# Modulation vectors of the later layers: from TensorE tiles to row sums on VectorE

## The reference, cut to what matters

```
mod_l = silu(c) @ w_mod[l] + b_mod[l]          # l = 0, 1; 1024 x 6144; the context uses c_ctx
sh1, sc1, g1, sh2, sc2, g2 = split(mod_l, 6)   # 1024 values each
h = rmsnorm(x) * (1 + sc1) + sh1
x = x + g1 * rmsnorm(mixer(h))
f = rmsnorm(x) * (1 + sc2) + sh2
x = x + g2 * rmsnorm((silu(f @ w_gate) * (f @ w_up)) @ w_down)
# the second pair of layers: the same with c_2, w_ada_2[0], w_ada_2[1] (1024 x 6144)
# and w_kv_ada_2 (1024 x 2048)
```

## Time and profile before

| | |
|---|---|
| Time, median of 3 runs | 2813.16 us (2807.47 to 2814.35) |
| Profiled execution, first to last instruction | 2812.3 us |
| PE busy | 2681.0 us (95%) |
| DVE busy | 2006.6 us (71%) |
| ACT busy | 1485.3 us (53%) |
| HBM traffic | 239 GB/s over the span |

### The profile page before, as it was taken

The page is one execution under the profiler, slowest core; times in us unless marked ns, Lnnn a source line. Parts: engine busy times, 40 slices in busy tenths (PEclk is TensorE's granted clock), DMA queues, the critical chain, the costliest instruction groups (busy, mean ns, idle before and its releaser), DMA issues.

```text
span 2812.3 us, 33306 instructions
## 1 busy us (share of the span) xinstructions
PE 2681.0 (95%) x13626; PEld 2140.2 (76%) x13626; DVE 2006.6 (71%) x2297; ACT 1485.3 (53%) x1663; POOL 121.7 (4%) x172
## 2 busy tenths in 40 slices
PE   7989999999999889999999999999999999999997
PEld 4767677777776667777777777888888888888886
DVE  4556565456457556558754667799999999999998
ACT  4322465245344244344643445677676677767775
POOL 3023100000000310000000000000000000000000
PEclk9989999999999899999899999999999999999999
DMA  7543556666545365652466433299999999999995
GB/s 272 181 154 120 195 195 213 215 229 215 195 168 192 135 222 197 239 187 72 150 210 235 162 105 116 98 364 368 353 369 365 356 358 366 359 358 361 369 365 206
DMA packets 283021, 674.26 MB, mean 240 GB/s; under 512 B 16774, under 2 KB 113158, under 8 KB 256752
## 3 DMA queue, kind: packets, MB, share of 16 engines
q1 hardware_dynamic: 277088, 664.34, 65.5%
q0 software_dynamic: 4912, 6.67, 0.9%
q10 hardware_dynamic: 864, 1.06, 0.1%
HBM read 670.93 MB, written 1.10 MB: 239 GB/s over the span
## 4 chain that ended last, share of the span: by engine, by line
PE 80%; DVE 10%; ACT 7%; DMA 2%; issue 1%; SPq 0%; POOL 0%; ACTq 0%; DVEq 0%; POOLq 0%
PE psum L560 22%; PE psum L562 21%; PE psum L561 21%; PE psum L76 8%; PE psum L394 3%; DVE wslot_r L570 2%; PE psum L1477 1%; DVE cacc L76 1%; PE psum L3009 1%; DMA first<-in_w_mod 1%; PE psum L1616 1%; PE psum L2041 1%; ACT whi_r L76 1%; DVE x L76 1%; DVE dslot_r L570 1%
## 5 line engine op out<-in xcount | busy, mean ns | idle before, releaser
L560 PE MATMUL psum<-whi_r,xhi_r 128*128 128x512 f32 (+1 forms) x752 | 295.2, 393 | 5.2 <-DVE dslot_r L570 2.1
L570 DVE TENSOR_TENSOR wslot_r<-wslot,whi_r 128x2048 fp32r<-128x2048 f32 (+1 forms) x114 | 255.6, 2252 | 50.1 <-ACT whi_r L76 48.9
L562 PE MATMUL psum<-whi_r,xlo_r 128*128 128x512 f32 (+1 forms) x752 | 288.8, 384 | 0.0
L561 PE MATMUL psum<-wslot_r,xhi_r 128*128 128x512 f32 (+1 forms) x736 | 282.4, 384 | 0.0
L570 DVE TENSOR_TENSOR dslot_r<-dslot,ld_hi_r 128x2048 fp32r<-128x2048 f32 x44 | 100.6, 2292 | 183.3 <-ACT ld_hi_r L76 183.3
L76 ACT ACTIVATE whi_r<-wslot 128x2048 fp32r<-128x2048 f32 (+1 forms) x114 | 212.2, 1874 | 23.5 <-DVE wslot L76 6.2
L570 DVE TENSOR_TENSOR ring_r<-ring,wide_r 128x2048 fp32r<-128x2048 f32 x84 | 192.0, 2288 | 18.1 <-ACT wide_r L2968 17.2
L570 DVE TENSOR_TENSOR wslot_r<-wslot,arena_r 128x2048 fp32r<-128x2048 f32 x85 | 194.2, 2288 | 14.3 <-ACT arena_r L2968 13.0
L570 DVE TENSOR_TENSOR wslot_r<-wslot,wide_r 128x2048 fp32r<-128x2048 f32 x83 | 189.7, 2288 | 17.0 <-ACT wide_r L2968 16.3
L570 DVE TENSOR_TENSOR ring_r<-ring,arena_r 128x2048 fp32r<-128x2048 f32 x84 | 191.7, 2287 | 12.9 <-ACT arena_r L2968 11.6
L2968 ACT ACTIVATE arena_r<-wslot 128x2048 fp32r<-128x2048 f32 x85 | 163.1, 1919 | 66.9 <-PE psum L562 60.1
(11 more groups left out here) (535 smaller groups left out, 6382.1 us busy)
## 6 DMA issues: line engine op xcount, KB each, us to landing
wslot<-in_moe_w_gate SPq DMA_DIRECT2D x29, 2048.0 KB, 7.9
ring<-in_moe_w_down SPq DMA_DIRECT2D x29, 2048.0 KB, 7.7
wslot<-in_moe_w_up SPq DMA_DIRECT2D x28, 2048.0 KB, 8.0
ring<-in_moe_w_up SPq DMA_DIRECT2D x28, 2048.0 KB, 8.1
ring<-in_moe_w_gate SPq DMA_DIRECT2D x27, 2048.0 KB, 7.9
wslot<-in_moe_w_down SPq DMA_DIRECT2D x27, 2048.0 KB, 7.7
dslot<-in_w_mod SPq DMA_DIRECT2D x35, 1024.0 KB, 4.8
wslot<-in_w_gate SPq DMA_DIRECT2D x66, 512.0 KB, 5.5
```

The costliest lines, as they stand in the source:

```text
L560: t.matmul(out_, hi, w_hi, start=start, stop=False)
L561: t.matmul(out_, hi, w_lo, start=False, stop=False)
L562: return t.matmul(out_, lo, w_hi, start=False, stop=stop)
L570: return v.tensor_tensor(one_pass(lo), src, one_pass(hi), ALU.subtract)
```

## The change

Of the 13 tiles the first five stay on PE: mod0 whole and the first two of mod1. The last third of mod1 (the scale and gate of the second half of layer 1, image tokens only, since the context is not updated there), ada0, kv and ada1 become 16 blocks of 1024 features. Their weights come from the host transposed: `w_dots` holds, for output feature p*8+k of a block, its 1024 weights in one row. On the chip one `tensor_tensor_reduce` on DVE multiplies 128 such rows by the conditioning vector, which stands on all partitions (`cond`, in the memory of stage), and sums along each row: one column of a block, 8 a block, 128 in all, each on 512 KB of weights.

A step of a dense line does two of them ahead of the first `beside` and two after the split of the first half of the tokens. The first line does 64, the second and third 32 each. The conditioning vector is broadcast by a POOL transfer and passed through Silu on ACT, once for c and once for c_2. The bias is added at the end of a block; gates go to DRAM as before. Nothing replaces the calls of `mod_step` in layer 1's projections, mixer and output projection.

```diff
+    def dot(limit):
+        n = dot_next[0]
+        if n not in dot_there or not broad[2]:
+            return
...
+        slot.reader = ve.put(v.tensor_tensor_reduce, slot.ap[:], slot.ap[:], cond, 1.0, 0.0, ALU.mult, ALU.add, column[:, k:k + 1],
+                             after=[dot_there.pop(n), broad[2]])
+        fetch_dot(limit)
+        if k == KD - 1:
...
+            summed = ve.op(v.tensor_tensor, column, column, dot_bias[:, n // KD, :], ALU.add)
...
+        if n == 2 * KD - 1:
+            broadcast_condition(i["c_2"][0])
...
+    def fetch_dot(limit):
+        n = dot_asked[0]
+        if n < limit:
+            dot_asked[0] += 1
+            slot = dot_slots[n % 2]
+            sp.wait(slot.reader)
+            nc.sync.dma_start(slot.ap[:], dot_rows[n // KD, :, n % KD, :]).then_inc(slot.sem, 16)
...
-    mod_tiles = [(job, j) for job in jobs for j in range(job[3])]
+    mod_tiles = [(job, j) for job in jobs[:2] for j in range(job[3])][:5]
...
-            def modulate(n):
+            def condition(n):
                 if n == 0:
-                    own_slot[0], line_slot.reader, allow_ahead[0] = line_slot, self.up_[0, 1], False
-                elif n > 1:
-                    while at_step[0] and mod_step() and at_step[0][0] != "half":
-                        pass
...
+                    for slot in dot_slots:
+                        slot.reader = self.up_[0, 1]
+                        fetch_dot(self.dots)
+                elif n < end - 1:
+                    for _ in range(2):
+                        dot(self.dots)
...
+                if n:
+                    condition(n)
                 beside(n)
-                if n:
-                    modulate(n)
                 self.up(n, 1)
                 self.high_w(n + 1, 1)
+                shape_condition()
                 self.gate(n, 1)
...
                 self.split_h(n, 0)
-                if n == 0:
-                    modulate(0)
+                condition(n)
                 beside(n)
...
         rounded = [high_part(0, half) for half in range(2)]
-        mod_step()
         low_part(0, 0, rounded[0])
-        settle()
+        if l == 0:
+            while mod_step():
+                pass
+            broadcast_condition(i["c"][0])
...
     finish_off(c0)
-    for _ in range(3):
-        mod_step()
     finish_off(c1)
```

More of the change, by code:

```diff
@@ L507, in load_columns @@
         for which, tile, at_ in parts:
-            mod_until(job, tile)
+            while (job, tile) not in known_cols:
+                assert mod_step()
             cols_for[which] = col_of[job][:, at_]
@@ L513, in ask_gates @@
     def ask_gates(job, *uses):
-        mod_until(job, 2 if max(blk for s, blk in uses) == 5 else 1)
+        while (job, 2 if max(blk for s, blk in uses) == 5 else 1) not in stored:
+            assert mod_step()
         grow_of.extend((job, s, blk) for s, blk in uses)
@@ L695, in build @@
     ld_hi = [at(f"ld_hi{u}", 16384 + 2048 * u, 2048) for u in range(2)]
-    line_slot = Slot(nc, "s_mod", at("mod_half", 18432, 2048))
+    dot_slots = [Slot(nc, f"s_dot{u}", at(f"dot{u}", 18432 + 1024 * u, 1024)) for u in range(2)]
+    s_broad, s_dotrow = nc.alloc_semaphore("s_broad"), nc.alloc_semaphore("s_dotrow")
+    cond = stage[:].rearrange("p u n -> p (u n)")
+    dot_gate = sb("dot_gate", [P, 2, 64])[:, :, 0:KD]
+    dot_there, dot_rows_n, gate_out, broad = {}, [0, 0], [None, None], [0, None, None]
@@ new lines, in build, with broadcast_condition, shape_condition @@
+    dot_next, dot_asked = [0], [0]
+    def broadcast_condition(src):
+        po.wait(*turned_out, (s_kept[0], kept_n[0]), (s_kept[1], kept_n[1]), ve.now())
+        nc.gpsimd.dma_start(cond, src.partition_broadcast(P)).then_inc(s_broad, 16)
+        broad[0] += 16
+        broad[1], broad[2] = (s_broad, broad[0]), None
+    def shape_condition():
+        if broad[1]:
+            broad[2] = ac.put(a.activation, cond, cond, ACT.Silu, after=[broad[1]])
+            broad[1] = None
+    def fetch_dot(limit):
[5 more added lines that the diff above has]
+            nc.sync.dma_start(slot.ap[:], dot_rows[n // KD, :, n % KD, :]).then_inc(slot.sem, 16)
+            slot.n += 16
+            dot_there[n] = (slot.sem, slot.n)
@@ L2627, in build @@
     cat4, keep, fetched = joint_mix(0)
-    line = Line(i["w_gate"][0], i["w_up"][0], i["w_down"][0], 2, whi, [keep, fetched[0]])
+    line = Line(i["w_gate"][0], i["w_up"][0], i["w_down"][0], 2, whi, [keep, fetched[0]], 8)
     there, last_gain = {CTX: {}, LAT: {}}, []
@@ L2667, in fetch_mixers @@
             fetch_tile((3, 0)[n])
-        else:
-            look_ahead(ahead[0] + 1)
     def stream(xh, xl, ready):
@@ L2687, in build @@
     cat4, keep, fetched = joint_mix(1)
-    line = Line(i["w_gate"][1], i["w_up"][1], i["w_down"][1], 1, [whi[1], whi[0]], [keep, fetched[0]], (3, 8))
+    line = Line(i["w_gate"][1], i["w_up"][1], i["w_down"][1], 1, [whi[1], whi[0]], [keep, fetched[0]], 12, (3, 8))
     there, last_gain = {LAT: {}}, []
@@ L3577 @@
     arrays, args = {}, {}
-    for name in NAMES:
-        a = _np.ascontiguousarray(inputs[name])
+    rows = [_np.asarray(w).T.reshape(-1, P, KD, D) for w in (inputs["w_mod"][1][:, 4 * D:], inputs["w_ada_2"][0], inputs["w_kv_ada_2"],
+                                                            inputs["w_ada_2"][1])]
+    packed = {"w_dots": _np.concatenate(rows, 0)}
+    for name in [n for n in NAMES if n not in ("w_ada_2", "w_kv_ada_2")] + ["w_dots"]:
+        a = _np.ascontiguousarray(packed[name] if name in packed else inputs[name])
         arrays["in_" + name] = a
```

60 lines of the change are left out of this document (31 added, 29 removed).

## The result

The changed kernel takes 2792.4 us (2787.7 to 2793.3, median of 4 runs) where the kernel before takes 2813.8 (2807.5 to 2816.2): a ratio of 0.991, interval 0.990 to 0.993. The forecast was 2750. The direction holds and the time lies inside the range, but two thirds of the gain are missing: 21.3 us by the two profiled executions (2812.3 less 2791.0) where 62.8 were worked out. Measured once more later, the same kernel took 2782.2 us (2781.1 to 2785.3), ratio 0.989 (0.988 to 0.991); the gap is then 32 us, half of the forecast.

The account below looks back on a forecast made before the run. PE bounds the dense lines; DVE and ACT make the chain in layer 1's projections. Savings of 70.8 us less 8.0 at the norm chains give 62.8 off 2812.3, so 2750 us, range 2724 to 2793 for 8 in 10.

Parts of the forecast that it names:

- The price at the norm chains: First line's steps with norm chains: row sums ahead of a split delay it, 0 to 20 us, taken as 8.0.
- the seven: Seven places at 370 to 480 and 600 to 720 us where PE waits 9.1 + 5.0 us for `split_h`.
- What goes in the first line: First dense line: 19 halves, 18.8 us, and two turns with stall and clock, 8.4; together 27.2 us saved.
- Second and third line: Dense lines two and three: halves and turns go, 10.6 and 9.0 us saved, no clock loss counted.
- that rival: Dense lines become bound by transfers: steps stay at 18.07 us, 34 halves give nothing, 2784 us; chance 0.07.
- a sign of being wrong: On DVE: the forecast is wrong if a row sum waits for its transfer; transfers were priced at 0.
- The row sum: On DVE: one row sum with its read takes 1.45 us, between bounds of 1.221 and 2.61.
- the slow row sum: Dense lines: at 2.61 us a row sum DVE becomes the bound, 2842 us; chance 0.08.
- Behind the first line: Last norm chain's transposes start 4.5 us sooner and a turn's delay of 1.5 goes; together 6.0 us saved.
- The mixer: Layer 1's mixer and output projection: 0 to 27.4 us saved, 16.0 taken from the chain's share on line 394.
- the mixer turns cold: Layer 1's mixer: without the halves the clock falls to 0.71, losing the 16 us and some 5 more, 2771; chance 0.14.
- since PE did other work under them: Mixer and output projection: ended waits for weights, 16.5% of the second stretch, counted at nothing.

Follow-up runs that it names:

- after_again: The changed kernel itself, unedited, measured once more later on another run's chip: 2782.2 us, ratio 0.989.
- e1_swap: Changed kernel with the two row sums behind the norm chain's piece (`beside`) instead of ahead, at both places of a dense-line step: 2777.1 us, ratio 0.986.
- e2b_noload: Changed kernel without the transfers of the row sums' weights, except the first two of each line; DVE's passes stay: 2786.3 us.
- e8_bnoload: Kernel before the change, its 29 modulation halves between first and second line multiplying a constant, without weight transfers: 4039.9 us, only stages ahead of the experts readable.
- e4_fill: Changed kernel with three idle identity matmuls where the kernel before issued a half of a modulation tile, in layer 1's projections and mixer: 2791.2 us.
- e6_place: Changed kernel, row sums behind the chain's piece, in the first line none and two in chain steps, two and three in steps 6 to 12: 2809.1 us.

## Why the prediction was wrong, point by point

41.5 us are missing between the two profiled executions (30.8 with after_again's profile of 2780.3). By the stretches of the first: first line 28.1, between the lines 7.3, layer 4 and the experts 8.4, less 1.9 gained in the second and third line and 0.4 at the start.

- **The price at the norm chains: the step that failed.** The prediction said that a pair of row sums ahead of a split "can add 0 or the whole 2.9 us, so 0 to 20 for the seven. I take 8.0, since DVE is partly idle there, waiting for ACT." The price was 33.7 us (410.0 less 376.3), above even its upper end. Two errors lie in it. DVE's idle time was taken for room, but DVE was idle *for* a result that ACT could begin only after a DVE instruction behind the row sums; idle time covers only what stands behind the instruction that starts the other engine, and only as much as the hole is long. e1_swap showed the first for 12.6 of the 33.7 us, and its step 3 the second. And the price was counted by PE's seven waits instead of by row sums: 36 of them stood in these steps, two pairs in nearly every step, and each cost 0.94 us.
- **What goes in the first line.** 27.2 us forecast. Without the chain steps' row sums it was 24.9 (401.2 less 376.3), near enough. A quiet step fell by 1.18 us, one with a turn by 5.45 (22.35 to 16.90, the half, the turn, the stall and the clock behind it).
- **Second and third line.** 10.6 and 9.0 forecast, 12.1 and 9.4 measured. Four row sums a step fitted, and the share of DMA came out at 0.87, and neither line was longer for its transfers: that rival falls by the steps of 16.9 us and by e2b_noload. Single row sums did wait for theirs, which the prediction named as a sign of being wrong, but it cost these lines nothing: step 1 of the second line is 2.5 us longer with the transfers than without (16.72 against 14.23), and the line is not.
- **The row sum.** 1.45 us taken, 1.219 measured, with a start every 1.14; the slow row sum falls. The rule of the Trainium skill on the scalar-tensor-tensor form (Vector Engine (DVE) Microarchitecture Reference, section 7), stretched to this operation, would have made it 2.6 us by an estimate; the measurement differs, for `tensor_tensor_reduce` with two float32 sources in SBUF at least.
- **Behind the first line.** 6.0 forecast. The timelines of ACT and DVE after the change, below, show the normalising of the last rows at 812.74 and their columns at 818.64, where the earlier trace rows had 805.22 and 815.71. That is 5.90 us against 10.49, so 4.6.

```profile
812.74 1.33 ACT L76 ACTIVATE ysb<-x,st 128x512 f32<-128x512 f32 x2 [0.92 <-DVE xbcT L76]
...
818.64 1.36 DVE L76 TENSOR_SCALAR xlo<-psum,col_mod 128x128 f32<-128x128 f32 x4
```

- **The mixer.** 16.0 forecast from the chain's share of line 394; 10.0 measured here (DVE's instructions stood 1.8 us later than before at the mixer's start and 8.2 earlier at the second line's), and 7.4 more between the lines in e1_swap, whose clock was 0.89. So "the mixer turns cold", given 0.14, happened in part: the 6 us that are missing of the 16 go with a clock of 0.81, though no run holds everything but the clock fixed. The cause was also put too simply. Of what went, weights and the waits for them were 7.1 (e8_bnoload), which the prediction had counted at nothing "since PE did other work under them", and PE's own work and the clock that it keeps up balanced (e4_fill put as much work back for 1.8 us, and the clock rose with it).
- **The rest.** 8.4 us in layer 4 and the experts have no term. 5.7 go with the granted clock of that execution, as after_again showed. The 2.7 in the experts stay open; every run of the changed kernel with the whole modulation has 1007 to 1010 there, against 1006.5.

## What to carry to other kernels

Idle time of an engine is room only for work that stands behind the instruction which starts the engine it waits for. Before work is put on an engine that "is partly idle", find in its timeline what releases each idle time and follow that back: if the releaser started from this same engine, put the new work behind that start, no longer than the idle time is and in a number that its buffers can feed. A price at a loop of two engines is counted by the instructions put on the loop, not by the waits that a third engine shows.

## What the hardware showed that was not expected

- The granted clock differs between executions over the same instructions, 0.77 to 0.89 in the mixer and 0.92 to 0.96 over layer 4's attention, and a stretch moved by up to 10 us with it; two measurements of one kernel stood 10 us apart (2792.4 and 2782.2). A forecast finer than that has to say which clock it assumes.
- A multiplication with a sum along the row costs DVE no more than the multiplication: 1.219 us against 1.221 for 128x1024. The read of the sum took 0.08, not the 0.164 of a small instruction, and the next row sum starts 1.14 us behind the one before.
- 28.7 us of waits for transfers on DVE cost nearly nothing where DVE has slack, while in e6_place 24.9 us of them within 85 us made each step 4 to 7 us longer.
